# Feed-forward up units as seven block products, from a ring of eight weight tiles, in four passes

## The chip, the cores and the metric

The kernel runs on one core of one Trainium2 chip. The time is the device time of one execution in microseconds (us), lower is better. PE is TensorE's matmul, PEld its weight load, DVE VectorE, ACT ScalarE, POOL GpSimd, SP SyncE.

## What is computed

Two layers of a streaming encoder for 512 prompt tokens and 32 sample tokens (544 in all), width 1024, everything in float32. Each layer is a half-step feed-forward, a mixer (pooling and retention branches) and a second half-step feed-forward:

```
mod = (silu(c) @ w_ada + b_ada)                       # 9 rows of 1024, per request group
h = rmsnorm(x, norm_g[0]) * (1 + mod[1]) + mod[0]
a, b = split(h @ w_up1)                                # w_up1: 1024 x 5632
x = x + 0.5 * mod[2] * ((silu(a) * b) @ w_down1)       # w_down1: 2816 x 1024
...                                                    # mixer, then the same with w_up2, w_down2
```

So there are four feed-forwards. Activations lie transposed: features on the 128 partitions, tokens along the free axis, as two halves of 272 tokens.

## The kernel before

**Precision.** Each float32 operand is cut in two parts of the shorter matmul format fp32r, `hi` and `lo = value - hi`, and each product is three matmuls: hi·hi, hi·lo, lo·hi (`product`, L447). Weights arrive by DMA in `raw[0]` and `raw[1]` (2048 floats per partition each, 1 MB in all 128). `split` makes a unit's parts: on ACT a copy to `w_hi` (L784), on DVE the difference `w_lo` (L1043).

**A feed-forward** is cut in two halves of the 2816 hidden features, 11 blocks of 128 each. An *up unit* j takes two 1024x128 blocks of weights (gate columns a, up columns b) and computes both for both token halves: 2 x 2 x 8 blocks of depth x 3 = 96 matmuls of 272 columns (`block_unit`, L484; the first unit of a feed-forward is `first_unit`, L465, which follows the depth blocks of h as they are made). ACT applies Silu to a (L855), DVE multiplies by b (L1189) and cuts the result u in `u_hi` (L1032) and `u_lo` (L1034). After the 11 up units of a half, 8 *down units* multiply u by 11x128 rows of w_down: 66 matmuls each, and DVE adds the result to x (`update_x`, L1159). Over a feed-forward there are 22 up units (2112 matmuls) and 16 down units (1056).

**The start of a feed-forward.** `make_h` (DVE, L1127) scales x, ACT adds the shift and rounds to `h_hi` (L811), for odd depth blocks ACT also writes the unrounded value (L816) and POOL makes `h_lo` (L376), for even ones DVE does (L1144).

**Shared work.** The modulation rows that later stages need (`w_ada`, 32 chunks of 512 columns after the first four) are computed beside the feed-forwards, in a fixed table of places: POOL issues the loads (`bring`, L405, DMA at L411), DVE takes one place of four multiply-adds of 512 columns (`ada_rows`, L1046; L1061, L1065) behind each token half of an up unit and each down unit, and PE sums a finished chunk with 16 short matmuls (`mods`, L507). The first feed-forward has 14 chunks, the second 6, the third 12, the fourth none.

**Order.** Each engine's queue is written out by hand and is executed in order; semaphores join them. SP loads the weights of unit n+2 when DVE has cut those of unit n (`load`, L272, wait on `w_split`, DMA at L277). In the feed-forwards POOL does only the odd `h_lo` at the start, the ada loads, and the `lo` parts of the squares for the next norm (`square_parts`, L383).

## Time and profile before

| what | value |
|---|---|
| three runs, median (lowest, highest) | 2634.83 us (2634.37 to 2636.46) |
| the profiled execution, its own time | 2635.26 us |
| its span, first to last instruction | 2633.4 us |
| mean granted TensorE clock | 0.977 of full |
| busy: PE, DVE, ACT, POOL | 94%, 56%, 28%, 9% |
| share of PE in the chain that ended last | 87% |

The profiled execution is 0.4 us over the median of the runs, and 1.9 us of it lie outside the span. A busy share is an average over stages; the chain shows what ended last in each. The duration of a matmul is its latency, of which several overlap; its price is taken from a stretch of many.

### The profile page before, as it was taken

The page shows a single profiled execution, that of the slowest core. Times are in us where ns is not written, and L with a number is a line of the kernel's source. Part 1 is how long each engine was busy: PE and PEld are TensorE (multiplying, and loading weights), DVE is VectorE, ACT ScalarE, POOL GpSimd, SP SyncE. Part 2 cuts the span into 40 slices and gives each one's busy share as a digit, 9 for nine tenths or more (in the row PEclk, how much of TensorE's full clock was granted, in tenths as well). Part 3 has the DMA queues.
Part 4 walks back from the last instruction along what each step waited for, and adds up shares of the span by engine and source line. Part 5 has one row for each costly group of instructions (what it writes and reads, how often), then busy time and mean ns, then how long its engine had stood idle before and what let it go on. Part 6 is the DMA issues. An engine that isn't in the chain of part 4 may idle for free.

```text
span 2633.4 us, 42638 instructions
## 1 busy us (share of the span) xinstructions
PE 2478.3 (94%) x19084; PEld 2412.5 (92%) x19084; DVE 1473.5 (56%) x2229; ACT 745.4 (28%) x892; POOL 241.6 (9%) x232
## 2 busy tenths in 40 slices
PE   7899999898899899999989999998989998999997
PEld 2899999888799899999989999998879998999997
DVE  1876776645745577534367667645555545434333
ACT  2311222433422431222241122234233234212222
POOL 1210111101000221000021001011000002000001
PEclk9899999999999999999999999999999998999998
DMA  6554654311123355332245455332112323323321
GB/s 203 182 156 136 174 163 126 100 51 53 55 73 105 96 152 158 99 97 76 77 121 168 143 163 164 101 92 78 42 47 73 94 77 87 83 75 106 82 67 56
DMA packets 401157, 279.91 MB, mean 106 GB/s; under 512 B 10090, under 2 KB 379218, under 8 KB 400846
## 3 DMA queue, kind: packets, MB, share of 16 engines
q1 hardware_dynamic: 379027, 204.73, 27.5%
q0 software_dynamic: 18432, 67.12, 8.4%
q10 hardware_dynamic: 3515, 5.34, 0.6%
q8 instruction: 150, 2.46, 0.4%
q14 instruction: 33, 0.27, 0.0%
HBM read 273.74 MB, written 3.40 MB: 105 GB/s over the span
## 4 chain that ended last, share of the span: by engine, by line
PE 87%; DVE 6%; ACT 4%; issue 1%; DMA 1%; POOL 1%; ACTq 0%; POOLq 0%; DVEq 0%
PE acc L452 76%; PE acc L477 3%; PE ps_mod L507 2%; PE acc L720 2%; ACT w_hi L784 1%; DVE w_lo L1043 1%; DVE rstd L1118 1%; PE ps_sum L605 1%; DMA ada_raw<-in_w_ada 1%; POOL h_lo L383 1%; DVE rstd L1310 1%; ACT h_hi L797 0%; PE ps_sum L540 0%; DMA x_in<-in_x_sample 0%; DVE tmp L1127 0%
## 5 line engine op out<-in xcount | busy, mean ns | idle before, releaser
L452 PE MATMUL acc<-h_hi,w_hi 128*128 128x272 f32 x3648 | 1055.2, 289 | 9.5 <-DVE q L1301 3.6
L452 PE MATMUL acc<-h_lo,w_hi 128*128 128x272 f32 x3648 | 1051.8, 288 | 0.0
L452 PE MATMUL acc<-h_hi,w_lo 128*128 128x272 f32 x3648 | 1051.4, 288 | 0.0
L1043 DVE TENSOR_TENSOR w_lo<-raw,w_hi 128x2048 fp32r<-128x2048 f32 x224 | 512.7, 2289 | 358.6 <-ACT w_hi L784 358.5
L452 PEld LDWEIGHTS acc<-h_hi,w_hi 128*128 128x128 f32 x3648 | 688.5, 189 | 12.8 <-issue 12.0
L452 PEld LDWEIGHTS acc<-h_lo,w_hi 128*128 128x128 f32 x3648 | 688.3, 189 | 0.0
L452 PEld LDWEIGHTS acc<-h_hi,w_lo 128*128 128x128 f32 x3648 | 686.9, 188 | 0.0
L784 ACT ACTIVATE w_hi<-raw 128x2048 fp32r<-128x2048 f32 x224 | 427.7, 1909 | 333.1 <-PE acc L452 223.3
L452 PE MATMUL acc<-u_hi,w_hi 128*128 128x272 f32 x1408 | 407.4, 289 | 14.2 <-DVE u_lo L1034 14.2
L452 PE MATMUL acc<-u_lo,w_hi 128*128 128x272 f32 x1408 | 408.8, 290 | 0.0
L452 PE MATMUL acc<-u_hi,w_lo 128*128 128x272 f32 x1408 | 408.0, 290 | 0.0
L855 ACT ACTIVATE acted<-acc 128x272 f32<-128x272 f32 x176 | 70.0, 398 | 848.2 <-PE acc L452 839.6
L1065 DVE SCALAR_TENSOR_TENSOR ada_acc<-ada_raw,c_by,ada_acc 128x512 f32<-128x512 f32 x448 | 307.5, 745 | 0.1
L1189 DVE TENSOR_TENSOR prod<-acted,acc 128x272 f32<-128x272 f32 x176 | 76.8, 436 | 395.2 <-ACT acted L855 395.0
L452 PEld LDWEIGHTS acc<-u_hi,w_hi 128*128 128x128 f32 x1408 | 268.8, 191 | 15.9 <-DVE u_lo L1034 15.9
L452 PEld LDWEIGHTS acc<-u_hi,w_lo 128*128 128x128 f32 x1408 | 268.7, 191 | 0.0
L452 PEld LDWEIGHTS acc<-u_lo,w_hi 128*128 128x128 f32 x1408 | 268.2, 190 | 0.0
L383 POOL TENSOR_TENSOR h_lo<-tmp,h_hi 128x544 fp32r<-128x544 f32 x56 | 84.4, 1510 | 1332.7 <-ACT h_hi L797 1332.5
L1159 DVE SCALAR_TENSOR_TENSOR x<-acc,coef,x 128x272 f32<-128x272 f32 (+2 forms) x288 | 99.2, 400 | 182.6 <-PE acc L452 172.2
L411 POOL DMA_DIRECT2D ada_raw<-in_w_ada x128 | 92.6, 723 | 709.6 <-DVE ada_acc L1065 696.5
L477 PE MATMUL acc<-h_hi,w_hi 128*128 128x272 f32 x192 | 61.7, 321 | 54.1 <-DVE h_lo L1144 44.0
L796 ACT ACTIVATE tmp<-x 128x544 f32<-128x544 f32 x56 | 36.7, 656 | 220.4 <-issue 197.8
(171 smaller groups left out, 2507.8 us busy)
## 6 DMA issues: line engine op xcount, KB each, us to landing
raw<-in_w_up SPq DMA_DIRECT2D x176, 512.0 KB, 5.3
ada_raw<-in_w_ada POOLq DMA_DIRECT2D x128, 512.0 KB, 4.1
raw<-in_w_in SPq DMA_DIRECT2D x72, 512.0 KB, 4.6
raw<-in_w_down SPq DMA_DIRECT2D x64, 384.0 KB, 4.2
raw<-in_w_down SPq DMA_DIRECT2D x64, 320.0 KB, 3.4
ada_raw<-in_w_ada SPq DMA_DIRECT2D x16, 512.0 KB, 4.6
raw<-in_w_o SPq DMA_DIRECT2D x32, 256.0 KB, 2.9
raw<-in_w_pool_out SPq DMA_DIRECT2D x16, 256.0 KB, 3.0
```

The costliest lines, as they stand in the source:

```text
L383: pool.tensor_tensor(h_lo[:, n, :], tmp[:, n % 2, :], h_hi[:, n, :].bitcast(F32), ALU.subtract)\
L411: pool.dma_start(ada_raw[slot][:, :, :], ada_source(l, c, kp)).then_inc(ada_landed[slot], 16)
L452: last = mm(out, ws(a, kk), xs(b, kk), start=(kk == 0 and n == 0), stop=(kk == nk - 1 and n == 2))
L477: last = mm(acc[:, 2 * hf + b, 0:HT], w[c][:, b, kk, :], (h_hi, h_lo)[d][:, kk, cols(hf)], start=(kk == 0 and n == 0), stop=(kk == KD - 1 ...
L507: last = mm(mod_cols(c // CHUNKS, (c % CHUNKS) * 4 + b, 1)[:, 0, g:g + 1], ada_acc[n % 2][:, g, b * P:(b + 1) * P], const[:, K_ONE:K_ONE + 1],
L720: last = mm(acc[:, 2 * b + hf, 0:HT], w[c][:, kk, b * P:(b + 1) * P], (m_hi, m_lo)[d][:, kk, cols(hf)], start=(kk == 0 and n == 0), stop=( ...
L784: act.activation(w_hi[p][:, :], raw[p][:, :], ACT.Copy).then_inc(w_rounded, 1)
L855: act.activation(acted[:, hf, 0, :], acc[:, 2 * hf, 0:HT], ACT.Silu).then_inc(acted_ok, 1)
L1043: dve.tensor_tensor(w_lo[p][:, :], raw[p][:, :], f(w_hi[p][:, :]), ALU.subtract).then_inc(w_split, 1)
L1065: last = dve.scalar_tensor_tensor(to[:, g, :], ada_raw[slot][:, e, :], by, to[:, g, :], ALU.mult, ALU.add)
L1159: last = dve.scalar_tensor_tensor(x[:, n, c:c + b - a], acc[:, 2 * p + hf, a:b], coef[:, s, 2, n, g:g + 1], x[:, n, c:c + b - a], ALU.mult ...
L1189: dve.tensor_tensor(prod[:, hf, 0, :], acted[:, hf, 0, :], acc[:, 2 * hf + 1, 0:HT], ALU.mult).then_inc(acc_free[hf], 1)
```

## The change

**Seven products.** For up units 2 to 21 of each feed-forward the 2x2 block product (depth halves k, k+4 of the weights' a and b columns against the two token halves of h) is made with seven block products in place of eight, after Winograd's form of Strassen's scheme. Each is 4 depth blocks x 3 = 12 matmuls of 272 columns, so a unit has 84 and not 96. Units 0 and 1 of each feed-forward stay whole (96 matmuls). Four of the seven use sums of weight blocks, which POOL makes for every unit: `s1`, `s2`, `s3`, `s4` (after, L632, L640, L651, L646), 128x512 each. Four use differences of token halves and depth halves of h, which POOL makes at the start of each feed-forward (`differences`, 16 operations of 272 columns), ACT rounds (`round_diff`) and DVE cuts (`low_diff`). The results are put together by DVE (`add`, `times` and products, five operations of 272 columns a unit) with three copies from PSUM by ACT; Silu now works in SBUF.

**Other moves.** `u_hi` is rounded by ACT (`round_u`) and `u_lo` made by POOL (`u_rest`, L657), where DVE did both. `make_full` takes the place of `make_h` for the feed-forwards: DVE scales by `rstd` alone, ACT applies scale and shift twice, once rounded and once not, for all eight depth blocks, and DVE makes all `h_lo`. `w_hi` and `w_lo` are a ring of eight tiles of 128x512 (`RING_T`): ACT rounds tile i once PE is done with tile i-8 (`rounds`), DVE cuts tile i+7 behind the work that follows on PE's tile i (`lows`). `raw` keeps two buffers; unit n+2 is loaded when the last tile of unit n is cut. A feed-forward has four passes of 6, 6, 5 and 5 up units, each followed by four down units of 256 columns (the 1056 matmuls are kept). The 32 ada chunks lie as 12, 10, 10 and 0, and their DVE work is dealt out within a unit (`rows_shared`: two places, 8 multiply-adds, in units 1 to 4 of the first two feed-forwards, one place in the others that have any). The constants' table is loaded again in each layer, on ACT's queue.

```diff
+PASSES = ((0, 6), (6, 12), (12, 17), (17, 22))
+UPS = FF // P
+DOWNS = 4
+JMAX = 6
...
+def turns(js):
+    out = [(js[0], 1), (js[0], 5)]
+    for i, j in enumerate(js):
+        follow = js[i + 1] if i + 1 < len(js) else None
+        out += [(j, 2), (j, 3), (j, 6)]
+        if follow is not None:
+            out.append((follow, 1))
+        out.append((j, 7))
+        if follow is not None:
+            out.append((follow, 5))
+        out.append((j, 4))
+    return out
...
+def rows_shared(f):
+    if f == 0:
+        return [0, 2, 2, 2, 2, 1] + [1] * 16, (2, 2, 2, 1)
+    if f == 1:
+        return [0, 2, 2, 2, 2, 1] + [1] * 16, (2, 1, 1, 1)
+    if f == 2:
+        return [0] + [1] * 21, (2, 1, 1, 1)
+    return [0] * UPS, (0, 0, 0, 0)
...
+            def load(p, first_part, second_part, last_tile=None):
                 if unit.n >= 2:
-                    sp.wait_ge(w_split, unit.at(-1))
+                    sp.wait_ge(*taken[unit.n - 2])
                 for dst, src in (first_part, second_part):
                     sp.dma_start(dst, src).then_inc(raw_landed[p], 16)
+                if last_tile is None:
+                    mid.step()
+                taken.append((w_split, mid.n) if last_tile is None else (tile_ready, last_tile - 3))
                 unit.step()
...
+            def up(f, w_up, j):
+                last = PLANS[f].tile[("up", j), 4 if j >= WHOLE else (1, 1)]
+                blocks(PLANS[f].load(("up", j)) % 2, w_up, f // 2, j * P, j * P + FF, last)
...
+            def differences(f):
...
+                for n in range(KD // 2):
+                    pool.wait_ge(h_rounded, (f // 2 * SETS + f % 2 * 2) * KD + 2 * n + 2)
+                    a1, b1 = h_full(n)[:, 0:HT], h_full(n)[:, HT:T]
+                    a2, b2 = h_full(n + 4)[:, 0:HT], h_full(n + 4)[:, HT:T]
+                    minus(d_sum[:, n, 2, :], b2, b1).then_inc(diff_step, 1)
+                    minus(d_sum[:, n, 0, :], b1, a1).then_inc(diff_made, 1)
+                    steps.step()
+                    pool.wait_ge(diff_step, steps.at())
+                    plus(d_sum[:, n, 1, :], d_sum[:, n, 2, :], a1).then_inc(diff_step, 1)
+                    steps.step()
+                    pool.wait_ge(diff_step, steps.at())
+                    minus(d_sum[:, n, 3, :], a2, d_sum[:, n, 1, :]).then_inc(diff_made, 1)
...
+                def s1(j):
+                    u = landed(j)
+                    if j == WHOLE:
+                        pool.wait_ge(h_ready[0], h_done)
+                    else:
+                        ready(plan.tile[("up", j - 1), 5])
+                        pool.wait_ge(s2_made, nth(j))
+                    pool.tensor_tensor(sum_of(1), raw_of(1, 0, u), raw_of(1, 1, u), ALU.add).then_inc(s1_made, 1)
...
+                def s2(j):
+                    u = plan.load(("up", j))
+                    if j > WHOLE:
+                        ready(plan.tile[("up", j - 1), 6])
+                        pool.wait_ge(s4_made, nth(j))
+                    pool.wait_ge(s1_made, nth(j) + 1)
+                    pool.tensor_tensor(sum_of(2), sum_of(1), raw_of(0, 0, u), ALU.subtract).then_inc(s2_made, 1)
...
+                def s4(j):
+                    u, i = plan.load(("up", j)), plan.tile[("up", j), 3]
+                    room(i)
+                    pool.wait_ge(s2_made, nth(j) + 1)
+                    pool.tensor_tensor(in_ring(w_sum, i), raw_of(0, 1, u), sum_of(2), ALU.subtract).then_inc(s4_made, 1)
+                def s3(j):
+                    u, i = plan.load(("up", j)), plan.tile[("up", j), 7]
+                    room(i)
+                    pool.tensor_tensor(in_ring(w_sum, i), raw_of(0, 0, u), raw_of(1, 0, u), ALU.subtract)\
+                        .then_inc(s3_made, 1)
...
+                def u_rest(j, hf, order):
+                    pool.wait_ge(u_rounded, f * 2 * UPS + 2 * j + order + 1)
+                    jj = j - [a for a, b in PASSES if a <= j < b][0]
+                    pool.tensor_tensor(u_lo[:, jj, hf * HT:(hf + 1) * HT], u_new(hf),
+                                       u_hi[:, jj, hf * HT:(hf + 1) * HT].bitcast(F32), ALU.subtract).then_inc(u_ready, 1)
...
+                            s1(js[n + 2])
+                        if n + 1 < len(js):
+                            s3(js[n + 1])
+                        if n + 2 < len(js):
+                            s2(js[n + 2])
+                        u_rest(j, 1, 0)
+                    u_rest(js[-1], 0, 1)
+                    for d in range(DOWNS):
+                        bring(f, places[0] + RING)
+                        places[0] += downs[d]
+                        if c == len(PASSES) - 1:
+                            square_parts((f // 2 * SETS + f % 2 * 2 + 1) * KD, 2 * d, 2 * d + 2)
+            square_parts(0, 0, KD)
             for layer in range(DEPTH):
-                odd_h(0, layer)
-                bring(layer, 0)
...
+            def seventh(f, j, p):
+                plan, first = PLANS[f], max(WHOLE, [a for a, b in PASSES if a <= j < b][0])
+                i = plan.tile[("up", j), p]
+                sum_a, sum_b, sum_c = banks(j)
+                out = {1: sum_a, 2: sum_b, 3: sum_c, 4: sum_a, 5: sum_c, 6: sum_a, 7: sum_a}[p]
+                if p == 1:
+                    if j - 2 >= first:
+                        pe.wait_ge(fold_done, plan.fold(j - 2, 5))
+                    elif first == WHOLE:
+                        pe.wait_ge(fold_done, plan.fold(j - 2, 2))
+                    elif j == first:
+                        pe.wait_ge(x_done, x_t.at(-1))
+                elif p == 2 and j == first:
+                    pe.wait_ge(x_done, x_t.at())
+                elif p == 6:
+                    pe.wait_ge(part_copied, plan.copied(j, 1))
+                elif p == 3:
+                    pe.wait_ge(part_copied, plan.copied(j, 2))
+                elif p == 7:
+                    pe.wait_ge(fold_done, plan.fold(j, 2))
+                elif p == 4:
+                    pe.wait_ge(fold_done, plan.fold(j, 3))
+                elif p == 5 and j == WHOLE:
+                    pe.wait_ge(diff_ready, 4 * f + 4)
+                pe.wait_ge(tile_ready, i - 3)
...
+            def round_full(s, kk):
+                scale_t.step()
+                act.wait_ge(scaled, scale_t.at())
+                for out in (h_hi[:, kk, :], h_full(kk)):
+                    for g, (a, b) in enumerate(SPANS):
+                        last = act.activation(out[:, a:b], h_full(kk)[:, a:b], ACT.Identity,
+                                              bias=coef[:, s, 0, kk, g:g + 1], scale=coef[:, s, 1, kk, g:g + 1])
+                last.then_inc(h_rounded, 1)
...
+            def rounds(f, until):
...
+                while ring.n <= until:
+                    own = plan if ring.n < plan.t0 + plan.tiles else PLANS[f + 1]
+                    nth = PLANS.index(own)
+                    i = ring.n
+                    unit, part = own.names[i - own.t0]
+                    u = own.load(unit)
+                    if i - RING_T in FREED:
+                        act.wait_ge(pe_done, FREED[i - RING_T])
+                    direct = unit[0] == "down" or unit[1] < WHOLE
+                    if direct or part in (1, 2, 4):
+                        act.wait_ge(raw_landed[u % 2], 32 * (LOADS0[nth] + u // 2 + 1))
+                    else:
+                        act.wait_ge({3: s4_made, 5: s1_made, 6: s2_made, 7: s3_made}[part],
+                                    nth * (UPS - WHOLE) + unit[1] - WHOLE + 1)
+                    n = tile_width(unit, part)
+                    act.activation(in_ring(w_hi, i, n), source(own, unit, part, i)[:, 0:n], ACT.Copy)\
+                        .then_inc(tile_rounded, 1)
+                    ring.step()
...
+            def lows(f_, until):
...
+                until = min(until, plan.t0 + plan.tiles + (plan.tiles if f_ == 1 else 0) - 1)
...
+                    unit_, part = own.names[i - own.t0]
...
+                        pass
+                    dve.wait_ge(tile_rounded, i - 3)
+                    dve.tensor_tensor(in_ring(w_lo, i, n), source(own, unit_, part, i)[:, 0:n], f(in_ring(w_hi, i, n)),
+                                      ALU.subtract).then_inc(tile_ready, 1)
...
+                    js = [j for j in range(j0, j1) if j >= WHOLE]
+                    for n, j in enumerate(js):
+                        sum_a, sum_b, sum_c = banks(j)
+                        k = ups[j]
+                        dve.wait_ge(pe_done, plan.event["up", j, 2])
+                        dve.wait_ge(part_copied, plan.copied(j, 1))
+                        add(gate_a(j), gate_a(j), sum_b).then_inc(fold_done, 1)
+                        used(("up", j), 2)
+                        ada_steps(todo, (0, 2, 3)[k])
+                        dve.wait_ge(pe_done, plan.event["up", j, 6])
+                        dve.wait_ge(part_copied, plan.copied(j, 3))
+                        add(gate_b, gate_b, sum_a).then_inc(fold_done, 1)
+                        used(("up", j), 6)
+                        ada_steps(todo, (0, 1, 2)[k])
+                        dve.wait_ge(pe_done, plan.event["up", j, 7])
+                        dve.wait_ge(u_ready, f_ * 2 * UPS + 2 * (j - 1) + (2 if j == WHOLE else 1))
+                        add(u_new(1), kept, sum_a).then_inc(fold_done, 1)
+                        dve.wait_ge(acted_ok, f_ * 2 * UPS + 2 * j + 2)
+                        dve.wait_ge(fold_done, plan.fold(j, 3))
+                        dve.tensor_tensor(u_new(1), u_new(1), gate_b, ALU.mult).then_inc(fold_done, 1)
+                        used(("up", j), 7)
+                        ada_steps(todo, (0, 0, 1)[k])
+                        dve.wait_ge(pe_done, plan.event["up", j, 4])
+                        dve.wait_ge(u_ready, f_ * 2 * UPS + 2 * (j - 1) + 2)
```

**GpSimd's queue.** In an up unit of the first feed-forward before, POOL has only the loads of ada rows; here the odd `h_lo`, these loads, and then the squares' parts:

```order
L376 TENSOR_TENSOR h_lo<-tmp,h_hi 128x544 [waits h_rounded]
L376 TENSOR_TENSOR h_lo<-prod,h_hi 128x544 [waits h_rounded]
L411 DMA ada_raw<-in_w_ada 128x2x512 [waits ada_used] x56
L383 TENSOR_TENSOR h_lo<-tmp,h_hi 128x544 [waits x_squared] x8
L376 TENSOR_TENSOR h_lo<-tmp,h_hi 128x544 [waits h_rounded]
```

The same queue after the change, one up unit of the second pass of the first feed-forward (`w_sum` and `prod` hold sums of weights):

```order
L657 TENSOR_TENSOR u_lo<-tmp,u_hi 128x272 [waits u_rounded] x2
L578 DMA ada_raw<-in_w_ada 128x2x512 [waits ada_used]
L646 TENSOR_TENSOR w_sum<-raw,prod 128x512 [waits s2_made,pe_done]
L632 TENSOR_TENSOR prod<-raw 128x512 [waits s2_made,tile_ready,raw_landed1]
L651 TENSOR_TENSOR w_sum<-raw 128x512 [waits pe_done]
L640 TENSOR_TENSOR prod<-prod,raw 128x512 [waits s1_made,s4_made,tile_ready]
```

Six computing operations stand in each unit where there were none, and the sum for tile 7 (L651) stands behind one that waits for the landing of the weights of the unit after next (L632).

**VectorE's queue.** One up unit of the first feed-forward before, from one cutting of the weights to the next:

```order
L1043 TENSOR_TENSOR w_lo<-raw,w_hi 128x2048
L1189 TENSOR_TENSOR prod<-acted,acc 128x272
L1032 CAST u_hi<-prod 128x272
L1034 TENSOR_TENSOR u_lo<-prod,u_hi 128x272
L1065 SCALAR_TENSOR_TENSOR ada_acc<-ada_raw,c_by,ada_acc 128x512 x4
```

(with the last four once more for the other token half), and after the change, one up unit of the second pass with one ada place:

```order
L1729 TENSOR_TENSOR acted<-acted,acc 128x272
L1618 TENSOR_TENSOR w_lo<-raw,w_hi 128x512
L1540 SCALAR_TENSOR_TENSOR ada_acc<-ada_raw,c_by,ada_acc 128x512 x2
L1729 TENSOR_TENSOR acted<-acted,ps_sum 128x272
L1618 TENSOR_TENSOR w_lo<-w_sum,w_hi 128x512
L1618 TENSOR_TENSOR w_lo<-prod,w_hi 128x512
L1540 SCALAR_TENSOR_TENSOR ada_acc<-ada_raw,c_by,ada_acc 128x512
L1729 TENSOR_TENSOR tmp<-acted,ps_sum 128x272
L1766 TENSOR_TENSOR tmp<-tmp,acted 128x272
```

followed by two cuts, the product at L1771, two cuts and one multiply-add: the one cut of 2048 columns has become seven of 512, the casts and `u_lo` are gone, and five operations of 272 columns wait for PE's products.

## Rows read from the trace of the kernel before

**Rows 1.** The page: busy time, share of the span and instructions of three engines.
```profile
PE 2478.3 (94%) x19084; PEld 2412.5 (92%) x19084; DVE 1473.5 (56%) x2229; ACT 745.4 (28%) x892; POOL 241.6 (9%) x232
```

**Rows 2.** Windows over the second and the fourth feed-forward: width, busy time, clock, DMA share, GB/s.
```profile
922.90:1340.40 417.50, 413.56 (x3285) 412.81 (x3286) 222.85 (x337) 103.99 (x118) 33.29 (x35) 0.99 0.39 111
2198.50:2598.80 400.30, 396.38 (x3124) 395.75 (x3125) 159.82 (x229) 100.87 (x113) 14.67 (x11) 0.99 0.28 77
```

**Rows 3.** The chain that ended last, in order of time: start, us, what.
```profile
148.04 24.21 PE acc L452 x192
...
172.25 1.68 PE ps_mod L507 x16
...
231.47 32.89 PE acc L452 x264
...
2213.24 120.58 PE acc L452 x960
```

**Rows 4.** Instructions in order of time, VectorE, one up unit of the first feed-forward.
```profile
115.72 0.44 DVE L1034 TENSOR_TENSOR u_lo<-prod,u_hi 128x272 fp32r<-128x272 f32 x1
116.08 2.73 DVE L1065 SCALAR_TENSOR_TENSOR ada_acc<-ada_raw,c_by,ada_acc 128x512 f32<-128x512 f32 x4
118.73 2.28 DVE L1043 TENSOR_TENSOR w_lo<-raw,w_hi 128x2048 fp32r<-128x2048 f32 x1
120.94 0.44 DVE L1189 TENSOR_TENSOR prod<-acted,acc 128x272 f32<-128x272 f32 x1
```

**Rows 5.** The same view of GpSimd, end of the first mixer.
```profile
899.13 2.38 POOL L383 TENSOR_TENSOR h_lo<-tmp,h_hi 128x544 fp32r<-128x544 f32 x1 [1.52 <-ACT h_hi L797]
902.60 1.38 POOL L383 TENSOR_TENSOR h_lo<-tmp,h_hi 128x544 fp32r<-128x544 f32 x1 [1.09 <-ACT h_hi L797]
```

**Rows 6.** The same view of VectorE, same stretch.
```profile
897.99 2.29 DVE L1043 TENSOR_TENSOR w_lo<-raw,w_hi 128x2048 fp32r<-128x2048 f32 x1 [1.49 <-ACT w_hi L784]
900.20 1.03 DVE L1159 SCALAR_TENSOR_TENSOR x<-acc,coef,x 128x272 f32<-128x272 f32 x3
```

**Rows 7.** The same view of GpSimd, start of the first feed-forward.
```profile
79.16 3.19 POOL L376 TENSOR_TENSOR h_lo<-tmp,h_hi 128x544 fp32r<-128x544 f32 x1 [2.58 <-ACT tmp L816]
84.94 1.35 POOL L376 TENSOR_TENSOR h_lo<-prod,h_hi 128x544 fp32r<-128x544 f32 x1 [2.58 <-ACT prod L816]
86.24 2.29 POOL L411 DMA_DIRECT2D ada_raw<-in_w_ada  x3
```

**Rows 8.** The same view of VectorE, same stretch.
```profile
77.22 0.90 DVE L1127 SCALAR_TENSOR_TENSOR prod<-x,coef,rstd 128x512 f32<-128x512 f32 x2
78.86 2.28 DVE L1043 TENSOR_TENSOR w_lo<-raw,w_hi 128x2048 fp32r<-128x2048 f32 x1
81.07 2.00 DVE L1127 SCALAR_TENSOR_TENSOR prod<-x,coef,rstd 128x512 f32<-128x512 f32 x2
```

**Rows 9.** The same view of GpSimd, sums of the first mixer.
```profile
555.56 1.14 POOL L398 TENSOR_TENSOR win<-pf 128x573 f32<-128x573 f32 x1 [18.39 <-DVE yp_lo L1034]
```

**Rows 10.** SyncE's DMA issues in order of time, then landing times in two stretches (90:220, 2220:2330).
```profile
2254.16 0.99 SPq L277 DMA_DIRECT2D raw<-in_w_up  x2
...
raw<-in_w_up SPq DMA_DIRECT2D x14, 512.0 KB, 5.9
...
raw<-in_w_up SPq DMA_DIRECT2D x12, 512.0 KB, 5.0
```

**Rows 11.** The chain at the start of the second feed-forward.
```profile
919.39 1.74 DVE tmp L1127 x4
...
937.40 30.36 PE acc L452 x240
```

**Rows 12.** ScalarE in order of time there, and in the page's groups.
```profile
922.00 0.92 ACT L816 ACTIVATE tmp<-tmp,coef 128x512 f32<-128x512 f32 x2
922.83 0.92 ACT L811 ACTIVATE h_hi<-prod,coef 128x512 fp32r<-128x512 f32 x2
...
L784 ACT ACTIVATE w_hi<-raw 128x2048 fp32r<-128x2048 f32 x224 | 427.7, 1909 | 333.1 <-PE acc L452 223.3
```

708 lines of the change are left out of this document (514 added, 194 removed).

## The prediction

> **What bounds the kernel now.** I read the page first, then windows over whole feed-forwards, then the chain, then single engines in order of time. PE is busy 94% of the span, DVE 56%, ACT 28%, POOL 9% [rows 1], and in the second and fourth feed-forward PE is busy 413.6 of 417.5 us and 396.4 of 400.3 [rows 2]: in these stages nothing but PE's number of matmuls counts. A matmul of 272 columns costs 120.58 us / 960 = 0.1256 us there [rows 3], at a granted clock of 0.99 of full over the stage [rows 2]; an up unit of 96 is 12.06 us. DVE's share is an average over feed-forwards with different shared work. In one with two ada places a unit, DVE's queue is already close to full: four multiply-adds take 2.65 us from start to start, the cut of 2048 columns 2.21 [rows 4], so a unit costs two times 2.65, 2.21 and two products with their parts, near 10 of 12.06 us. So a change that shortens PE's unit and adds to DVE must be read on DVE.
>
> **What it saves on PE.** 80 units (20 in each feed-forward) lose 12 matmuls each: 960 x 0.1256 = 120.6 us. A unit becomes 84 x 0.1256 = 10.55 us. Down units keep their 1056 matmuls. The ada sums stay 32 times 1.68 us [rows 3] and only lie elsewhere.
>
> **What it costs on DVE, in its own time.** From start to start a two-input operation of 272 columns takes 0.36 us and one of 2048 2.21 [rows 4], which is 1.04 ns a column, so 0.61 us for 512. A unit has seven cuts (4.3), five operations of 272 (1.8), and 0, 4 or 8 multiply-adds (0, 2.65, 5.3): 6.1, 8.7 or 11.4 us with no, one or two ada places. Against 10.55 us of PE this fits for the first two, taken alone. Casts and `u_lo` have left DVE; that is counted.
>
> **What POOL adds, and takes from DVE.** POOL has four sums of 512 columns and two `u_lo` of 272 in a unit. A sum of 573 columns took 1.14 us [rows 9], 2.0 ns a column, so 1.02 us for 512; a difference of 544 with fp32r output took 1.35 [rows 7], which would make it 1.27. `u_lo` is half of 1.35, 0.68. That is 5.4 to 6.4 us, and with one issue of an ada load (2.29 us for three [rows 7]) 6.2 to 7.2: POOL alone also fits in 10.55.
>
> But POOL and DVE do not run side by side. POOL's 544-column operation takes 1.38 us when DVE does nothing with it, and 2.38 when it starts inside DVE's cut of 2048 columns [rows 5, 6]: started at 899.13, it waits until that cut ends at 900.28 and runs its 1.2 us behind it, while DVE's update of x from PSUM keeps its 1.03 us. In the other direction, DVE's scaling pair takes 0.90 us and takes 2.00 when POOL's operation has got in first [rows 7, 8]. So an operation of DVE with both inputs in SBUF and one of POOL exclude each other, and each 1.35 us of POOL held DVE up for 1.10, 81%. The Trainium skill's page SBUF — State Buffer, section Who interferes with whom, says that a VectorE instruction with two SBUF inputs contends with a GpSimd instruction that reads SBUF and that the second to issue blocks fully. By that rule the ada multiply-adds would be held up too, which no row here shows (during them POOL only issued DMAs); without them in the lock the sum would be some 30 us lower, and I follow the rule's side because the scaling, of the same operation and with the same two inputs in SBUF, was held up [rows 8].
>
> In a unit POOL then holds DVE up for 0.81 x (5.4 to 6.4) = 4.4 to 5.2 us. The last unit of a pass has no sums and the first one's begin beside the down units, so 5/6 of the sums count: 4.2. Of DVE's time some four fifths go to operations with two SBUF inputs (cuts, ada, one product); the other operations read PSUM. I take 3.4 us. DVE's unit is then 9.3, **12.1** and 14.9 us.
>
> The page GPSIMD Engine Reference, section Elementwise — side-by-side cycle accounting, gives 4497 ns for a two-input add of 2048 columns, an estimate of 1.12 us for 512; by it the 80 units would come out about 17 us later than by 1.02. It lies inside the two ends from the rows.
>
> **A loop through the weights' buffers.** The load of unit n+2 starts when the last tile of unit n is cut. POOL makes the sum for tile 7 of unit n+1 behind the first sum of unit n+2, which waits for that landing; and the last tile of unit n+1 is cut behind tile 7. One turn, with no ada: issue of the second DMA 0.5 and landing 5.0 [rows 10], two sums 2.3, rounding 0.5 (a quarter of 1.91 [rows 12]), three cuts and one product on DVE 2.2, and 1.5 for POOL and DVE in each other's way: 12.0 us. With ada loads the landing is 5.9 [rows 10] and DVE is later: 13.2. It holds for four units of six (the first two are loaded ahead, in the down stage), and some 2 us of slack is there at the start of a pass.
>
> So per unit: with no ada (4 x 12.0 + 2 x 10.55 - 2) / 6 = 11.2; with one place (4 x 13.2 + 2 x 12.1 - 2) / 6 = 12.5; with two 14.9. Nearest rows for the ends: PE's own 10.55 below, and above the sum of DVE's and all of POOL's time, 11.5 / 14.1 / 16.8.
>
> **The start of a feed-forward.** Before, from the first scaling to the second unit 18.0 us [rows 11]. ACT rounds a depth block in 0.83 us [rows 12] and now does 16 of these, 13.3 us, and three of 1088 columns of differences, near 1.0 each; ahead and behind lie a scaling and a cut (0.8 each) and the last 24 matmuls, 3.0: 21 us, and POOL's 16 differences stand in DVE's way: 22. That is +4, four times. Unit 1 has 8 multiply-adds behind its products in the first two feed-forwards, which push the first addition of unit 2 and with it PE's seventh product: +4 each. Ends: 0 and 20 us for all of these together on one side, 45 on the other.
>
> **Down units.** A pair of column blocks is 72 matmuls, 9.0 us (60 and 7.5 in the last two passes; 66 matmuls stood in 8.2 before, four units in 32.89 [rows 3]). DVE has three cuts 1.8, two updates of x of 1.03 [rows 6] and, in the first feed-forward, 8 multiply-adds 5.3: 9.2. That is late by 0.2 to 1.7: +10 in all. The four pass changes against two half changes: the last down products begin with the blocks of u that are ready, so nothing. The constants' table and its DMA are hidden by the last down units; if not, 7 us or less.
>
> **Sum**, against the profiled execution's 2635.3 us: 20 units x (11.2 - 12.06) = -17; 54 x (12.5 - 12.06) = +24; 6 x (14.9 - 12.06) = +17; starts +16; unit 1 twice +8; down units +10: +58, so 2693. The profiled execution is 0.4 us over the median, which I leave out.
>
> **Rivals.**
> *A: PE stays the bound.* If POOL's sums find the gaps of DVE (it reads PSUM, or waits, some 3 us a unit) and the loop is shorter, a unit is 10.55: -120.6, starts +16, down units +10: 2541. For: each engine alone fits in 10.55 us in 74 of the 80 units, and a ring of eight tiles lets the cuts run 10 us ahead. Against: PE's seventh and fourth products wait for additions that stand in the same DVE queue as cuts and multiply-adds, so the ring cannot absorb DVE's lateness. It decides where POOL holds DVE up less than 1.9 us a unit. Chance 0.17.
> *B: the lock is milder,* each POOL operation costs DVE half of what I take, and the loop is 1 us shorter: units 10.7, 11.7 and 13.2: -27 - 19 + 7 + 24 = -15, 2620. Chance 0.12.
> *C: more is serial.* DVE and PE wait for each other in turn (four points in a unit where DVE waits for PE and two where PE waits for DVE), and POOL's time adds in full: 11.5, 14.1, 16.8: -11 + 110 + 28 + 45 = 2807. Chance 0.13.
> *D: the change does not do what it says:* fewer products are not made. The order of PE's instructions shows 960 rows less; I give it nothing.
>
> **Chances.** The forecast, 2640 to 2770, has 0.58. A measurement of this kernel tells 0.2% (5 us) from no change. Faster: A, and most of B, 0.28; within 0.2%: 0.04; slower 0.68. The range reaches from inside B to inside C, 2560 to 2790: it leaves out A and half of C.
>
> **What would show it.** Right: in the fourth feed-forward (no ada) PE has almost no waits in the first two units of a pass and then waits for `tile_ready`; in the third its units take 12 to 13 us; POOL's sums of 512 last 1.0 when DVE is idle and 1.5 or more beside it, and DVE's cuts of 512 show a mean well over 0.7 us, with single ones of 1.5. The first unit ends 4 us later. Wrong: cuts of 512 at 0.7 us throughout, PE busy over 98% in the up stages, and the fourth feed-forward under 375 us. If that one gains 25 us and the others lose, the lock is right and the loop is not; if all four lose the same, neither ada nor the lock is the cause but the chain of additions.

## The result and the profile after

The change makes the kernel slower: 2850.02 us (median of four runs, 2845.34 to 2854.88) against 2635.45 before (2634.37 to 2636.46), a ratio of 1.0814, 95% interval 1.0792 to 1.0837. The forecast of 2693 had the direction right and the size wrong (+215 us, not +58), and the time lies outside its range. The profiled execution has a span of 2843.5 us, 210.1 more than before.

Engines, busy time and share, and the chain of waits by engine, from the page of the kernel after (of before: [rows 1], and PE with 87% of the chain):

```profile
PE 2469.2 (87%) x18124; PEld 2371.1 (83%) x18124; DVE 1966.9 (69%) x2925; ACT 1080.9 (38%) x1988; POOL 941.2 (33%) x776
...
PE 44%; DVE 24%; issue 10%; ACT 8%; DMA 7%; POOL 6%; SPq 0%; ACTq 0%; POOLq 0%; DVEq 0%
```

The 960 matmuls are gone, but PE is no longer what ends last in more than half of the span. Windows over the second and the fourth feed-forward after (columns as in [rows 2]):

```profile
982.50:1475.60 493.10, 424.34 (x3106) 415.21 (x3107) 397.03 (x584) 189.99 (x394) 220.74 (x187) 0.93 0.38 112
2390.00:2817.00 427.00, 386.66 (x2948) 379.44 (x2949) 265.69 (x408) 187.96 (x389) 191.35 (x147) 0.97 0.25 72
```

In the second feed-forward PE is busy 424.3 of 493.1 us, where it was busy 413.6 of 417.5 [rows 2]: longer, with 20 times 12 matmuls less and four more chunks' ada sums. The granted clock over this stretch is 0.93 and was 0.99. Scaled by the clock the busy time fell by some 15 us, where the count of matmuls asks for 23 less (both are estimates from these rows); the difference was not taken apart.

The groups of VectorE and GpSimd that share operands in SBUF, from the groups by shape (last column: idle time before, and what ended it):

```profile
L1618 DVE TENSOR_TENSOR w_lo<-raw,w_hi 128x512 fp32r<-128x512 f32 x432 | 375.4, 884 | 54.0 <-ACT w_hi L1222 53.9
L1540 DVE SCALAR_TENSOR_TENSOR ada_acc<-ada_raw,c_by,ada_acc 128x512 f32<-128x512 f32 x448 | 412.4, 955 | 1.1
L632 POOL TENSOR_TENSOR prod<-raw 128x512 f32<-128x512 f32 x80 | 114.6, 1432 | 264.2 <-DMA raw<-in_w_up 262.6 <-issue 1.4
L651 POOL TENSOR_TENSOR w_sum<-raw 128x512 f32<-128x512 f32 x80 | 127.7, 1596 | 17.5 <-PE acc L928 17.5
L657 POOL TENSOR_TENSOR u_lo<-tmp,u_hi 128x272 fp32r<-128x272 f32 x176 | 183.6, 1045 | 308.1 <-ACT u_hi L1270 308.1
```

A cut of 512 columns takes 884 ns in the mean and a multiply-add 955; alone they take 0.68 and 0.74 us (below). GpSimd's four sums take 1417 to 1596 ns in the mean. One unit of the second feed-forward with one ada place, VectorE in order of time:

```profile
1182.54 0.68 DVE L1618 TENSOR_TENSOR w_lo<-raw,w_hi 128x512 fp32r<-128x512 f32 x1
1183.15 2.69 DVE L1540 SCALAR_TENSOR_TENSOR ada_acc<-ada_raw,c_by,ada_acc 128x512 f32<-128x512 f32 x2
...
1187.82 1.85 DVE L1540 SCALAR_TENSOR_TENSOR ada_acc<-ada_raw,c_by,ada_acc 128x512 f32<-128x512 f32 x1
1189.59 0.42 DVE L1729 TENSOR_TENSOR tmp<-acted,ps_sum 128x272 f32<-128x272 f32 x1
1190.12 0.98 DVE L1766 TENSOR_TENSOR tmp<-tmp,acted 128x272 f32<-128x272 f32 x1
1191.02 1.78 DVE L1618 TENSOR_TENSOR w_lo<-raw,w_hi 128x512 fp32r<-128x512 f32 x1
1192.73 1.25 DVE L1618 TENSOR_TENSOR w_lo<-w_sum,w_hi 128x512 fp32r<-128x512 f32 x1
...
1195.46 1.25 DVE L1540 SCALAR_TENSOR_TENSOR ada_acc<-ada_raw,c_by,ada_acc 128x512 f32<-128x512 f32 x1
...
1196.98 0.68 DVE L1618 TENSOR_TENSOR w_lo<-raw,w_hi 128x512 fp32r<-128x512 f32 x1
```

and GpSimd beside it:

```profile
1183.32 1.30 POOL L646 TENSOR_TENSOR w_sum<-raw,prod 128x512 f32<-128x512 f32 x1
1187.83 1.29 POOL L632 TENSOR_TENSOR prod<-raw 128x512 f32<-128x512 f32 x1 [3.21 <-DMA raw<-in_w_up]
1189.08 1.72 POOL L651 TENSOR_TENSOR w_sum<-raw 128x512 f32<-128x512 f32 x1
1190.76 1.49 POOL L640 TENSOR_TENSOR prod<-prod,raw 128x512 f32<-128x512 f32 x1
1192.20 1.23 POOL L657 TENSOR_TENSOR u_lo<-tmp,u_hi 128x272 fp32r<-128x272 f32 x1
1194.88 1.29 POOL L657 TENSOR_TENSOR u_lo<-tmp,u_hi 128x272 fp32r<-128x272 f32 x1 [1.44 <-ACT u_hi L1270]
```

The unit takes 14.4 us (1182.54 to 1196.98). Against their times alone six of VectorE's operations are longer by 1.3, 1.1, 0.5, 1.1, 0.6 and 0.5 us, each time while one of GpSimd's runs: 5.1 us. The products that read PSUM (0.42) are never longer. GpSimd's sum costs 1.30 and u_lo 0.77 where they need not wait, 6.7 us a unit, so VectorE is held up for 76% of it.

**Where the time is.** The first and the last down matmul of each pass in PE's rows cut a feed-forward into up stretches and down stretches. In us, for three kernels (whole_units is an experiment below: the change without the seven products and with `u_lo` on VectorE, as fast as before):

| stretch | whole_units | after | narrow_sums |
|---|---|---|---|
| reciprocal to first down unit, 1st feed-forward | 121.6 | 151.0 | 135.0 |
| the same, 2nd, 3rd | 86.8, 84.9 | 112.2, 109.0 | 103.3, 96.1 |
| the same, 4th | 83.2 | 92.9 | 84.8 |
| up units of passes 2 to 4, 1st, 2nd, 3rd (16 each) | 203.0, 199.5, 199.4 | 245.1, 242.1, 242.7 | 194.4, 194.0, 196.1 |
| the same, 4th | 192.2 | 202.4 | 176.4 |
| all down units, 3rd and 4th | 144.7, 137.2 | 140.5, 133.0 | 140.6, 133.1 |

Summed up, after loses 128 us in 48 units beside ada work, 10 in the 16 of the fourth feed-forward and 89 in the first passes, and gains 15 in the down stretches (6 of them in the first two feed-forwards, not in the table): 212, and the spans differ by 209 (2843.5 and 2634.2).

### The profile page after: what moved, and what is told of

The parts are those of the page before. It is cut to its first block, busy times and chain, and to the rows that moved or that the text cites. A ratio compares the mean times of both kernels' runs of the same rounds, so it can differ in the third digit from the quotient of the medians.

```text
span 2843.5 us, 44785 instructions
## 1 busy us (share of the span) xinstructions
PE 2469.2 (87%) x18124; PEld 2371.1 (83%) x18124; DVE 1966.9 (69%) x2925; ACT 1080.9 (38%) x1988; POOL 941.2 (33%) x776
## 4 chain that ended last, share of the span: by engine, by line
PE 44%; DVE 24%; issue 10%; ACT 8%; DMA 7%; POOL 6%; SPq 0%; ACTq 0%; POOLq 0%; DVEq 0%
PE acc L735 19%; PE acc L928 13%; DVE ada_acc L1540 7%; DVE w_lo L1618 6%; DMA raw<-in_w_up 5%; PE ps_sum L735 3%; ACT w_hi L1222 3%; POOL prod L632 2%; PE ps_misc L735 2%; PE acc L1100 2%; POOL w_sum L651 1%; DVE acted L1729 1%; PE acc L760 1%; DVE x L1690 1%; ACT h_hi L1191 1%
## 5 line engine op out<-in xcount | busy, mean ns | idle before, releaser
L735 PE MATMUL acc<-h_hi,w_hi 128*128 128x272 f32 x1600 | 471.0, 294 | 50.0 <-ACT acted L1275 39.3
L735 PE MATMUL acc<-h_lo,w_hi 128*128 128x272 f32 x1600 | 466.2, 291 | 0.0
L735 PE MATMUL acc<-h_hi,w_lo 128*128 128x272 f32 x1600 | 466.1, 291 | 0.0
L1618 DVE TENSOR_TENSOR w_lo<-raw,w_hi 128x512 fp32r<-128x512 f32 (+1 forms) x464 | 392.4, 864 | 59.0 <-ACT w_hi L1222 59.0
L1540 DVE SCALAR_TENSOR_TENSOR ada_acc<-ada_raw,c_by,ada_acc 128x512 f32<-128x512 f32 x448 | 412.4, 955 | 1.1
L1222 ACT ACTIVATE w_hi<-raw 128x512 fp32r<-128x512 f32 (+1 forms) x464 | 270.7, 605 | 324.2 <-PE acc L928 215.3
L735 PEld LDWEIGHTS acc<-h_hi,w_hi 128*128 128x128 f32 x1600 | 306.0, 191 | 57.8 <-ACT acted L1275 43.3
L1515 DVE TENSOR_TENSOR w_lo<-raw,w_hi 128x2048 fp32r<-128x2048 f32 x72 | 164.8, 2290 | 223.7 <-ACT w_hi L1163 223.7
L735 PEld LDWEIGHTS acc<-h_lo,w_hi 128*128 128x128 f32 x1600 | 306.3, 191 | 0.0
L735 PEld LDWEIGHTS acc<-h_hi,w_lo 128*128 128x128 f32 x1600 | 305.8, 191 | 0.0
L657 POOL TENSOR_TENSOR u_lo<-tmp,u_hi 128x272 fp32r<-128x272 f32 x176 | 183.6, 1045 | 308.1 <-ACT u_hi L1270 308.1
L632 POOL TENSOR_TENSOR prod<-raw 128x512 f32<-128x512 f32 x80 | 114.6, 1432 | 264.2 <-DMA raw<-in_w_up 262.6
```

The source lines that it names most:

```text
L632: pool.tensor_tensor(sum_of(1), raw_of(1, 0, u), raw_of(1, 1, u), ALU.add).then_inc(s1_made, 1)
L657: pool.tensor_tensor(u_lo[:, jj, hf * HT:(hf + 1) * HT], u_new(hf), u_hi[:, jj, hf * HT:(hf + 1) * HT].bitcast(F32), ALU.subtract).then_in ...
L735: last = mm(out, ws(a, kk), xs(b, kk), start=(begin and kk == 0 and n == 0), stop=(end and kk == nk - 1 and n == 2), skip_group_check=onto)
L1222: act.activation(in_ring(w_hi, i, n), source(own, unit, part, i)[:, 0:n], ACT.Copy)\
L1515: dve.tensor_tensor(w_lo_at[p], raw[p][:, :], f(w_hi_at[p]), ALU.subtract).then_inc(w_split, 1)
L1540: last = dve.scalar_tensor_tensor(to[:, g, :], ada_raw[slot][:, e, :], by, to[:, g, :], ALU.mult, ALU.add)
```

## The experiments

Theory: an operation of GpSimd and one of VectorE with its tensor inputs in SBUF exclude each other, and VectorE's queue, lengthened so, sets the units. First rival: a loop through the buffers of `raw` (landing, sums, roundings, last cut, load). Second: the chain of additions between PE, ACT and VectorE.

**s3_first**: GpSimd makes the sum for tile 7 ahead of the one that waits for the landing.

```diff
+                    s3(js[0])
                     s1(js[1])
-                    s3(js[0])
...
+                        if n + 1 < len(js):
+                            s3(js[n + 1])
                         if n + 2 < len(js):
                             s1(js[n + 2])
-                        if n + 1 < len(js):
-                            s3(js[n + 1])
```

> The changed kernel with POOL's sum for tile 7 of a unit put ahead of the first sum of the next unit but one, so that it no longer waits for that unit's landing. Loop theory (the way load, landing, two sums, rounding, cuts, next load sets the unit): a turn loses one sum, 1.3 us; in the fourth feed-forward units fall from 12.93 to about 11.6 us, in the others (14.4 us) less, since DVE is full there; 2820 to 2835 against 2850. Lock theory alone (POOL's time in DVE's way sets every unit): no change over 5 us.

Measured: 2818.71 us (2814.9 to 2822.18), ratio to before 1.0684 [1.0666, 1.0702], 1 us below the expected range. In the middle units of passes 2 to 4 of the fourth feed-forward the chain of waits of after is the forecast loop:

```profile
2528.51 1.29 POOL prod L632
2529.80 1.69 POOL w_sum L651
...
2531.57 0.64 ACT w_hi L1222
...
2533.18 0.41 DVE tmp L1771
2533.59 0.77 issue
2534.36 1.27 DVE w_lo L1618
...
2535.65 0.37 SPq L439
...
2536.06 5.31 DMA raw<-in_w_up
...
2541.44 1.29 POOL prod L632
...
2567.37 1.30 POOL prod L632
...
2591.80 36.09 PE acc L928 x288
```

Its turn is 12.93 us (2528.51 to 2541.44). Three turns stand in the second pass and two each in the third and fourth, 90 of the 202 us of these up units. The last two units of a pass (24 us, here 2567.37 to 2591.80) are not the loop: there the chain goes from GpSimd's sums and `u_lo` through roundings, additions and PE's products in turn. In s3_first, GpSimd in order of time, the same sum comes after 11.73:

```profile
2517.36 1.29 POOL L632 TENSOR_TENSOR prod<-raw 128x512 f32<-128x512 f32 x1 [2.80 <-DMA raw<-in_w_up]
...
2529.09 1.30 POOL L632 TENSOR_TENSOR prod<-raw 128x512 f32<-128x512 f32 x1 [2.99 <-DMA raw<-in_w_up]
```

The fourth feed-forward, from its reciprocal to the next, falls from 435.0 to 420.9 us. So the loop bounds units there; in the others (501.4 to 497.4 and 500.1 to 495.1 in the second and third) it is a small part.

**second_input_psum**: the second input of cuts, multiply-adds and one product is a zeroed bank of PSUM, from unit 4 of each feed-forward to its last up unit, down units of the first three passes included. The values are then not those of the reference; shapes and order stay. The edit for the cuts:

```diff
-                    dve.tensor_tensor(in_ring(w_lo, i, n), source(own, unit_, part, i)[:, 0:n], f(in_ring(w_hi, i, n)),
+                    second = ps_sum[:, 1, 0:n] if free[0] else f(in_ring(w_hi, i, n))
+                    dve.tensor_tensor(in_ring(w_lo, i, n), source(own, unit_, part, i)[:, 0:n], second,
                                       ALU.subtract).then_inc(tile_ready, 1)
```

> From up unit 4 of each feed-forward to the last down units but the last pass's, DVE's cuts, ada multiply-adds and the product of the two gates take their second input from an unused PSUM bank in place of SBUF (wrong values, same sizes and counts), so that they have one SBUF input; POOL's work and all waits stay. Lock theory: DVE's cuts of 512 fall from 0.88 us mean to 0.68 and multiply-adds from 0.95 to 0.75, a unit with one ada place from 14.4 to about 12.3 us, the fourth feed-forward by under 1 us a unit; 2850 falls to about 2730. Rival, DVE's own work and the loop set the unit: within 20 us of 2850.

Measured: 2732.86 us (two runs), ratio 1.0363 [1.0343, 1.0384]: 117 us less than after by the operand's place alone. The groups of this kernel, with the freed form and the one left as it was:

```profile
L1621 DVE TENSOR_TENSOR w_lo<-raw,ps_sum 128x512 fp32r<-128x512 f32 x348 | 232.1, 681 | 51.9 <-ACT w_hi L1222 51.9
...
L1621 DVE TENSOR_TENSOR w_lo<-raw,w_hi 128x512 fp32r<-128x512 f32 x84 | 78.2, 953 | 10.7 <-ACT w_hi L1222 10.7
```

681 ns against 953 in one execution. The fourth feed-forward takes 419.4 us and not 435.0. In the second pass of the third feed-forward a unit takes 13.1 us where it took 15.1 (up stretch over six units).

**narrow_ada**: the 448 ada multiply-adds of L1540 are 16 columns wide; the modulation rows are then not those of the reference.

```diff
-                        last = dve.scalar_tensor_tensor(to[:, g, :], ada_raw[slot][:, e, :], by, to[:, g, :],
+                        last = dve.scalar_tensor_tensor(to[:, g, 0:16], ada_raw[slot][:, e, 0:16], by, to[:, g, 0:16],
                                                         ALU.mult, ALU.add)
```

> DVE's ada multiply-adds (448) on 16 columns in place of 512, loads unchanged. Lock and full DVE: the first three feed-forwards fall to the fourth one's 12.9 us a unit and their down units are free of DVE; about 2700. Loop theory alone: it stays at 2820 or more, since no step of the loop is an ada operation.

Measured: 2784.38 us (two runs), ratio 1.0559 [1.0538, 1.058]. Neither expectation held; it falls between. The 16-column operations, 0.22 us alone, are still held up for whole sums of GpSimd. VectorE and then GpSimd of this kernel:

```profile
1166.35 0.22 DVE L1540 SCALAR_TENSOR_TENSOR ada_acc<-ada_raw,c_by,ada_acc 128x16 f32<-128x16 f32 x1
...
1167.44 2.90 DVE L1540 SCALAR_TENSOR_TENSOR ada_acc<-ada_raw,c_by,ada_acc 128x16 f32<-128x16 f32 x2
```

```profile
1167.62 1.30 POOL L646 TENSOR_TENSOR w_sum<-raw,prod 128x512 f32<-128x512 f32 x1
1168.84 1.32 POOL L651 TENSOR_TENSOR w_sum<-raw 128x512 f32<-128x512 f32 x1
```

So what a wait costs is GpSimd's length, whatever VectorE's operation has to do. The fourth feed-forward, which has no ada work, is unchanged (434.6 us). In the other three the up units of passes 2 to 4 take 14.1 to 14.6 us, where the first expectation had the 12.9 of the fourth; what makes up this difference beyond the waits just shown and PE's ada sums is open.

**narrow_sums**: GpSimd's four sums of a unit are 16 columns wide; for two of the four, roundings and cuts then read `raw` (four of the seven products are not those of the reference). One of the four edits:

```diff
-                    pool.tensor_tensor(sum_of(1), raw_of(1, 0, u), raw_of(1, 1, u), ALU.add).then_inc(s1_made, 1)
+                    pool.tensor_tensor(sum_of(1)[:, 0:16], raw_of(1, 0, u)[:, 0:16], raw_of(1, 1, u)[:, 0:16], ALU.add).then_inc(s1_made, 1)
```

> POOL's four sums of weights on 16 columns in place of 512 (ACT and DVE read the plain weights for tiles 3 and 7), everything else the same. Lock and loop together: both ends of the matter shrink, the fourth feed-forward's units reach PE's 10.55 us, the others about 11; about 2620, near the kernel before. Rival, the chain of additions between PE and DVE sets the units: no less than 2780.

Measured: 2631.36 us (2624.88 to 2632.51), ratio 0.9971 [0.9958, 0.9984]. 11 us above what was expected. The width of GpSimd's sums alone is worth 219 us. PE, ScalarE and VectorE keep all their additions and the waits between them, so the second rival, which asked for 2780 or more, is out. The table above shows where: units of passes 2 to 4 are at 12.1 to 12.3 us in the first three feed-forwards (PE's 10.55 and ada sums of some 0.4, with waits left), where about 11 was expected, and 11.0 in the fourth; the first passes still lose.

**dve_sums** and **dve_sums_u_lo**: VectorE makes the four sums, each one tile ahead of its cut; in the second kernel it also makes `u_lo`. The outputs are the same as before. The call, in the loop of the cuts:

```diff
+                    sum_for(f_, i + 1)
                     dve.wait_ge(tile_rounded, i - 3)
                     dve.tensor_tensor(in_ring(w_lo, i, n), ...
```

> The four sums of a unit are made by VectorE (0.68 us each, 2.7 us a unit, one tile ahead of its cut) and not by GpSimd (1.3 us each, 5.3 us a unit); u_lo stays on GpSimd. The output is the same. If GpSimd's time comes off VectorE's (the lock), VectorE gains 5.3 and pays 2.7 a unit: a unit with one ada place 14.4 -> 12.5 to 13.7 us, a unit of the fourth feed-forward 12.9 -> 10.6 to 11.5: 2720 to 2780 us. If GpSimd and VectorE ran side by side and VectorE were merely late, 2.7 us more on it for 74 units would make it slower than the changed kernel: 2900 us or more.

> As dve_sums, and u_lo also on VectorE (two operations of 0.42 us a unit, where GpSimd takes 0.77 us each); in the up stages GpSimd then does nothing but issue loads. The output is the same. VectorE's own time with one place: seven cuts 4.8, four sums 2.7, five operations and two u_lo 2.8, four multiply-adds 3.0: 13.3 us at most, 10.3 without a place. Lock: faster than dve_sums by 0 to 40 us, 2700 to 2760 us, cuts at 0.68 and multiply-adds at 0.74 us throughout. No lock: slower than dve_sums by some 60 us (0.84 us in 80 units).

Measured: 2711.71 us (2709.09 to 2717.1), ratio 1.0286 [1.0271, 1.0302], and 2687.5 (2681.31 to 2689.03), 1.0188 [1.0172, 1.0203]. Giving VectorE, the busiest engine behind PE, 2.7 us more work a unit made the kernel 138 us faster, and 0.9 us more another 24. dve_sums came out 8 us below its range and dve_sums_u_lo 12 below. Groups of dve_sums_u_lo:

```profile
L1473 DVE SCALAR_TENSOR_TENSOR ada_acc<-ada_raw,c_by,ada_acc 128x512 f32<-128x512 f32 x448 | 322.6, 755 | 1.1
...
L1580 DVE TENSOR_TENSOR w_lo<-prod,w_hi 128x512 fp32r<-128x512 f32 x160 | 109.9, 687 | 21.7 <-ACT w_hi L1155 21.7
...
L1551 DVE TENSOR_TENSOR prod<-raw 128x512 f32<-128x512 f32 x80 | 54.7, 684 | 1.1 <-DMA raw<-in_w_up 1.1
```

A sum is 684 ns here, half of GpSimd's 1.30 us, and the multiply-adds and cuts are back near their times alone. The sums also left the loop's slower engine, so the 138 us are the worth of hold and loop together.

**s3_first_psum**: both edits at once (the values are not those of the reference, as in second_input_psum).

> The reordered GpSimd queue of s3_first together with second_input_psum (the second input of cuts, multiply-adds and one product read from a zeroed PSUM bank, wrong values, same shapes). If loop and lock are separate causes, their gains add: -31 and -117 make 2850 -> 2702, 2695 to 2715 us. If they are one cause (the loop is only long because VectorE is held up), little is left for the reordering: 2725 to 2735 us.

Measured: 2695.73 us (2692.56 to 2699.58), ratio 1.022 [1.0203, 1.0238]. The gains add: 31.3 and 117.2 make 148.5, measured 154.3. So loop and hold are two causes.

**before_with_sums**: the kernel before, with six GpSimd operations a unit on constants; no other engine waits for them.

```diff
+                    for n in range(6):
+                        w = 512 if n < 4 else HT
+                        pool.tensor_tensor(dead[:, 0:w], const[:, K_MASK:K_MASK + w], const[:, K_MASK + 512:K_MASK + 512 + w],
+                                           ALU.add).then_inc(dead_ok, 1)
...
+                    for n in range(2):
+                        if todo:
+                            one()
```

> The kernel before, with six GpSimd operations added to each up unit: four sums of 512 and two of 272 columns of constants into a tile that nobody reads, begun when ScalarE's Silu of the unit is done. Nothing waits for them, so only the lock can cost time. VectorE's unit before was near 10 us with two ada places; with 5 to 6 us of GpSimd on top of it it passes PE's 12.06. Lock: the units with two ada places go to 14 or 15 us, the fourth feed-forward stays (VectorE has 5 us of work there): 2680 to 2780 us in all, VectorE's multiply-adds at 0.9 us or more beside them. No lock: 2635 to 2642 us.

Measured: 2741.28 us (2740.47 to 2744.23), ratio 1.0398 [1.0383, 1.0414]. 104 us are lost with no wait for these operations on any other engine. The ada loads stand behind them in GpSimd's queue, but VectorE waited only 0.1 us for ada rows in the whole execution. The first and third feed-forwards take 520.8 and 476.9 us (480.3 and 439.8 before), the fourth 419.0 (419.9). VectorE's group of four multiply-adds beside the last four of five GpSimd operations that run from 189.34 to 196.12, and a group free of them:

```profile
190.85 5.82 DVE L1100 SCALAR_TENSOR_TENSOR ada_acc<-ada_raw,c_by,ada_acc 128x512 f32<-128x512 f32 x4
...
197.75 2.73 DVE L1100 SCALAR_TENSOR_TENSOR ada_acc<-ada_raw,c_by,ada_acc 128x512 f32<-128x512 f32 x4
```

**whole_units**: all of the change but the seven products: every unit whole, no sums, no differences, `u_lo` on VectorE.

```diff
-WHOLE = 2
...
+WHOLES = (22, 22, 22, 22)
```

> Everything of the change but the seven products: all 22 units of each feed-forward are whole (96 matmuls in four tiles), no sums, no differences, u_lo on VectorE; passes, ring of eight tiles, places of the ada work and the start by make_full stay. PE has the 19084 matmuls of before. VectorE needs 2.7 + 0.9 + 0.9 + 3.0 = 7.5 us in a unit with one place, 10.5 with two. If the seven products are the whole cost and the whole gain, this is the kernel before with somewhat later starts: 2636 to 2655 us. If ring, passes or places of ada work cost by themselves, it is 2670 us or more.

Measured: 2635.62 us (11 runs, 2633.3 to 2636.45), ratio 0.9992 [0.9983, 1.0]. Passes, ring, double rounding at the start and places of ada work cost nothing together. All 215 us belong to the seven products, what feeds them, and `u_lo` on GpSimd.

**copy_first**: dve_sums_u_lo with ScalarE's copy of the third product ahead of roundings that wait for VectorE's next sum, and at the start the copies of unit 2 ahead of four roundings. The first of the two edits:

```diff
-                        used(("up", j), 2)
                         copy(j, 3)
+                        used(("up", j), 2)
```

> dve_sums_u_lo with two places in ScalarE's queue changed: the copy of the third product stands ahead of the roundings that wait for VectorE's next sum, and in the first two units the copies of unit 2 stand ahead of four roundings. In the trace of dve_sums_u_lo the end of the fourth feed-forward's units was set by DVE w_sum, ACT w_hi, ACT acted, DVE acted in turn, and PE waited 5.7 us for the copies at unit 2. If this order is what is left in units without ada work, that feed-forward goes from 407 to 398 to 402 us; where there are ada places VectorE's own 13.3 us stay the bound, so the others gain 0 to 8 us each: 2660 to 2680 us. If VectorE's work is the bound there too, no change: 2687 us.

Measured: 2696.71 us (2696.3 to 2697.5), ratio 1.0228 [1.0213, 1.0243]. Worse by 9 us, 3 of them in the fourth feed-forward (407.2 to 410.4, where 398 to 402 was expected), 5 in the first and 4 in the third: a miss. That a wait stands in the chain of waits did not mean that moving it helps. What the new order delays was not traced.

**seven_in_fourth** and **seven_in_fourth_2**: seven products in the fourth feed-forward alone, with sums and `u_lo` on VectorE; the others whole. The second keeps ScalarE's first order.

```diff
-WHOLE = 2
...
+WHOLES = (22, 22, 22, 2)
```

> Seven products only in the fourth feed-forward, the one without ada work, with sums and u_lo on VectorE and ScalarE's copies first; the other three have whole units as in whole_units. The output is the same. First three feed-forwards as in whole_units, the fourth 398 to 402 us where before it took 419.9: about 20 us less than whole_units, 2612 to 2635 us, and the first version faster than before: 0.99 to 0.998 of it. If the fourth one's gain is lost in its start: 2636 us or more.

> seven_in_fourth with ScalarE's queue in its first order (as in dve_sums_u_lo, where the fourth feed-forward took 407.2 us against 410.4 with the copies first). Everything else equal. If the order of the copies is what cost those 3 us, the fourth feed-forward takes 406 to 408 us and the kernel 2619 to 2626 us; if the 3 us were chance, 410 us and 2627 us.

Measured: 2626.94 us (2619.0 to 2629.56), ratio 0.996 [0.9948, 0.9972], and 2624.09 (2619.04 to 2628.76), 0.9954 [0.9941, 0.9968]. Both outputs are those of before. Both whole times lie in the expected ranges. The fourth feed-forward took 410.8 and 407.4 us: the 398 to 402 that the first expected, from copy_first's forecast, was missed, and the 3 us of the order came back. The two whole times overlap. The second is the fastest version that computes the reference: 12 us under before, less than half a per cent.

## Why the prediction was wrong in size

The mechanism was forecast, its size was not. Of the 155 us that the stretches of the table lie above the forecast's terms, 107 are in passes 2 to 4 of the first three feed-forwards (+128 measured, 48 x 0.44 = +21 forecast), 49 in the first passes (+89, some +40), 24 in passes 2 to 4 of the fourth (+10, 16 x (11.2 - 12.06) = -14), and -25 in the down units (-15, +10). The steps, as the prediction put them:

- **PE's saving and the price of a unit: right.** The 960 matmuls less are there (18124 against 19084 on the page). narrow_sums keeps the 84 matmuls a unit and needs 176.4 us for 16 units of the fourth feed-forward, 11.0 each with the waits that are left, against 192.2 for whole ones.
- **"Each 1.35 us of POOL held DVE up for 1.10, 81%": right.** The unit above shows 76% of 6.7 us. That the multiply-adds are held up too, which no row of before showed, holds: 955 ns in after, 755 without sums on GpSimd, 5.82 us for four in before_with_sums. By the Trainium skill, page SBUF — State Buffer, section Who interferes with whom, this is the pair of two SBUF inputs on VectorE and a GpSimd read; every run here agrees, the operand in PSUM (681 against 953 ns) most directly.
- **"I take 3.4 us": wrong, and the main fault.** This is the time by which GpSimd's work in a unit holds VectorE up. It came of 5/6 (last unit of a pass without sums) and 4/5 (share of VectorE's time in the lock) on top of 81%, and of sums at 1.02 to 1.27 us. Measured in a middle unit: 5.1 us, 76% of GpSimd's time with no further discount. Why the discounts did not come true is read from the queues and not tested: VectorE's holds little but cuts and multiply-adds, so nearly every operation of GpSimd meets one. The sum itself is 1.27 to 1.30 us alone; of the prediction's two ends for it, 1.02 (from 1.14 for 573 columns [rows 9]) was too low and 1.27 (from 1.35 for 544 [rows 7]) was right. Units with one place went to 14.4 us, not 12.1 to 12.5. Rival C had this term right (14.1 us) and a chance of 0.13.
- **The loop, 12.0 us: right as a mechanism, 0.9 short.** Seven turns of 12.8 to 13.0 stand in the chain of the fourth feed-forward. No single term is the fault: "two sums 2.3" are 2.6 at their time alone, issue and landing with the gaps behind them 5.8 and not 5.5, the rounding 0.7 and not 0.5. The 1.5 for both engines in each other's way came to 1.6 (0.4 on the second sum, 1.2 on three cuts). What surrounds the turns was further off: the last two units of a pass, put at PE's 10.55, take 12.1 each, and the 2 us of slack at the start of a pass are not seen. In a pass of six (4 x 12.9 + 2 x 12.1) / 6 makes 12.7 a unit, which is what the up units of passes 2 to 4 took there, and not 11.2.
- **Starts, "+4, four times" and "+4 each" for unit 1: a term is missing.** The +4 itself was near: in the fourth feed-forward unit 1 ends 35.2 us after the first scaling; before, it begins 18.3 us after it (2194.96 to 2213.24), and with 12.06 ends after 30.3: +4.9. What was given nothing is the step from whole units to units of seven products. The chain there, from PE's last whole products on:

```profile
2419.12 6.02 PE ps_sum L735 x48
...
2425.96 0.63 POOL u_lo L657
...
2427.24 1.22 POOL u_lo L657
2428.46 1.69 POOL prod L632
2430.14 1.23 POOL w_sum L651
...
2431.99 0.61 ACT w_hi L1222
2432.61 0.58 ACT acted L1275 x2
...
2433.23 5.81 PE acc L735 x24
```

Unit 2's sum for tile 7 stands on GpSimd behind `u_lo` of unit 1 and a sum of unit 3, and ScalarE's copies of unit 2 behind its rounding. PE's windows of this place, the waiting and what follows:

```profile
2425.10:2433.30 8.20, 4.64 (x38) 4.42 (x36) 4.17 (x6) 3.91 (x9) 7.20 (x6) 0.94 0.01 3
2433.30:2447.00 13.70, 13.70 (x88) 13.70 (x89) 9.13 (x12) 6.53 (x14) 6.14 (x5) 0.78 0.27 77
```

PE waits 3.6 us, and over the next 13.7 the granted clock is 0.78 of full: part of it at the lower of its two levels, 1.2 and not 2.4 GHz. 24 matmuls take 5.81 us there; 24 of the whole units just before took 3.02. "+4 each" for unit 1 was not measured by itself. Against whole_units, narrow_sums still loses 16 and 11 us in the first passes of the second and third feed-forwards, dve_sums_u_lo 20 and 11; how these divide between transition, differences and ada work is open.
- **Down units, +10: wrong.** 140.5 and 133.0 us for 16 of them; 1056 matmuls by 0.1256 are 132.6, and the rest is ada sums. DVE's 9.2 against PE's 9.0 never showed; that the ring runs ahead would explain it, and was not tested.
- **Clock: left out of the sum.** It had PE at 0.99 of full throughout; in after it is 0.93 in the second feed-forward. No experiment sets a price on it apart from the waits that it follows.

Of the signs named beforehand, these came: sums longer beside VectorE than alone (1.4 to 1.6 in the mean; alone 1.3 and not 1.0), cuts over 0.7 us with single ones of 1.78, the first unit's end 4.9 us later (4 forecast). Not so: units of the third at 12 to 13 us; they took 15.1 to 15.2 with ada sums.

## What to carry to other kernels

Work given to GpSimd to spare VectorE spared it nothing here: a sum cost VectorE about 1 us on GpSimd and 0.68 on itself, and making the four sums itself gave 138 us. Before crediting an engine with "it fits beside", add GpSimd's whole time to VectorE's in a stage where VectorE's queue is nearly full, without discounts for chance; and test it on the kernel before, with added operations that no other engine waits for. A scheme that trades PE's work for elementwise work pays only where the other engines have room: here in the stage without ada work, 12 us of the 30 (240 x 0.1256) that the seven products save PE there.
